# Sample cross-attention on four 32-column quarters of TensorE, two heads at a time

## The reference, cut to what matters

```python
D_MODEL, SEQ, DEPTH, DEC_BATCH, DEC_SEQ = 1024, 256, 2, 8, 8
N_MEM, XA_HEADS, XA_HEAD_DIM = 256, 4, 256

def cross_attend(h, mem_k, mem_v, w_q, w_o):
    b, L, _ = h.shape
    q = (h @ w_q).reshape(b, L, XA_HEADS, XA_HEAD_DIM)
    s = jnp.einsum('blhd,bmhd->bhlm', q, mem_k).astype(jnp.float32) * (XA_HEAD_DIM ** -0.5)
    p = jax.nn.softmax(s, axis=-1).astype(mem_v.dtype)
    o = jnp.einsum('bhlm,bmhd->blhd', p, mem_v).reshape(b, L, D_MODEL)
    return o @ w_o
```

## Time and profile before

| | |
|---|---|
| median of 3 runs | 2010.04 us (2007.63 to 2014.47) |
| profiled execution | 2015.52 us, of which the span 2013.6 us |
| mean granted TensorE clock in it | 0.933 of 2.4 GHz |
| PE busy | 1895.2 us (94%) |
| DMA | 382.66 MB, mean 190 GB/s |

### The profile page before, as it was taken

How to read it: one execution, slowest core, us unless ns; L and a number is a source line. 1 busy time by engine, 2 the same in 40 slices (tenths; PEclk the granted TensorE clock), 3 DMA queues, 4 the chain that set the end, 5 groups by cost and what they waited for, 6 DMA issues and landing times.

```text
span 2013.6 us, 18677 instructions
## 1 busy us (share of the span) xinstructions
PE 1895.2 (94%) x7908; PEld 1165.9 (58%) x7908; DVE 504.6 (25%) x1062; ACT 301.0 (15%) x666; POOL 32.1 (2%) x34
## 2 busy tenths in 40 slices
PE   7999999999999989999899999999999989999996
PEld 5766676666666534444367666766766664444342
DVE  0028544421102111111201276345011030211112
ACT  2114210311111010000111132104012011000001
POOL 0000000001000000000000000000010000000000
PEclk9999999899998689998999999999999967999898
DMA  6332226532453377877822422265325425887683
GB/s 253 125 114 99 84 105 221 213 141 94 164 216 122 135 283 310 329 321 292 334 71 101 163 87 71 97 235 224 131 99 209 167 84 208 331 332 298 270 324 143
DMA packets 28680, 382.66 MB, mean 190 GB/s; under 512 B 3184, under 2 KB 3568, under 8 KB 3888
## 3 DMA queue, kind: packets, MB, share of 16 engines
q1 hardware_dynamic: 25040, 356.69, 45.9%
q0 software_dynamic: 3552, 24.71, 3.0%
HBM read 356.67 MB, written 24.71 MB: 189 GB/s over the span
## 4 chain that ended last, share of the span: by engine, by line
PE 87%; DVE 4%; ACT 4%; DVEq 2%; issue 1%; DMA 1%; ACTq 0%; POOL 0%; SPq 0%; POOLq 0%
PE psum L471 27%; PE psum L925 11%; PE psum L910 7%; PE psum L945 7%; PE psum L749 7%; PE psum L970 4%; PE psum L808 3%; PE psum L838 3%; PE psum L478 2%; PE psum L712 2%; PE psum L689 2%; PE psum L709 2%; DVE work L1452 2%; PE psum L699 2%; PE psum L876 1%
## 5 line engine op out<-in xcount | busy, mean ns | idle before, releaser
L471 PE MATMUL psum<-h,ring 128*128 128x320 f32 x1920 | 535.2, 439 | 7.7 <-DVE h L1377 6.3
L471 PEld LDWEIGHTS psum<-h,ring 128*128 128x128 f32 x1920 | 367.9, 193 | 165.3 <-issue 18.0
L925 PE MATMUL psum<-ring,work 128*64 128x512 f32 x1024 | 237.6, 609 | 1.5 <-ACT work L1325 1.4
L925 PEld LDWEIGHTS psum<-ring,work 128*64 128x64 f32 x1024 | 70.4, 139 | 142.3 <-issue 136.8
L910 PE MATMUL psum<-work 128*128 128x128 f32 (+1 forms) x768 | 150.4, 329 | 1.4 <-ACT work L1312 1.4
L910 PEld LDWEIGHTS psum<-work 128*128 128x128 f32 (+1 forms) x768 | 114.1, 204 | 55.4 <-issue 29.4
L945 PE MATMUL psum<-ring,work 128*64 128x512 f32 x512 | 142.2, 718 | 1.1 <-ACT work L1337 1.1
L749 PE MATMUL psum<-work,ring 128*128 128x320 f32 x512 | 138.3, 433 | 0.9 <-ACT work L1099 0.9
L471 PE MATMUL psum<-mem,ring 128*128 128x256 f32 x512 | 122.8, 394 | 4.0 <-ACT work L1099 4.0
L749 PEld LDWEIGHTS psum<-work,ring 128*128 128x128 f32 x512 | 97.1, 190 | 42.0 <-ACT work L1099 1.8
L471 PEld LDWEIGHTS psum<-mem,ring 128*128 128x128 f32 x512 | 98.4, 197 | 21.2 <-issue 7.1
(11 more groups left out here) (240 smaller groups left out, 1453.2 us busy)
## 6 DMA issues: line engine op xcount, KB each, us to landing
ring<-stream SPq DMA_DIRECT2D x168, 2048.0 KB, 9.0
st_out<-states_out POOLq DMA_DIRECT2D x18, 1024.0 KB, 9.4
mk_out<-k_mem POOLq DMA_DIRECT2D x2, 1024.0 KB, 6.1
mv_out<-work POOLq DMA_DIRECT2D x2, 1024.0 KB, 5.6
cst<-consts SPq DMA_DIRECT2D x1, 1456.0 KB, 22.0
x<-x_in SPq DMA_DIRECT2D x1, 1280.0 KB, 5.8
y_out<-h POOLq DMA_DIRECT2D x2, 640.0 KB, 3.2
mem<-mem_in SPq DMA_DIRECT2D x1, 1024.0 KB, 23.9
```

The costliest lines, as they stand in the source:

```text
L471: mm = pe.matmul(out, w[:, a:a + P], rhs[:, j, :], start=(j == 0), stop=(j == KD - 1))
L925: mm = pe.matmul(psum[ab * CAP:(ab + 1) * CAP, up, :], h_packed[:, p % 2, k, ab * CAP:(ab + 1) * CAP], w[:, a:a + BANK], start=(k == 0), s ...
```

## The change

The eight batches become two groups (`GB`) of four. Batch b of a group is multiplied by 8 stationary columns straight from the queries, and its result goes to PSUM rows 32b to 32b + 7, that is to the b-th quarter of 32 columns of the array; `q_own`, `prob_own` and POOL's two memsets go. Each group is treated as a tile of 128 tokens in softmax and in the transposes (`XT` = 4 tiles: two of the prompt, two of the sample). The stage is cut in two halves `hp` of two heads each, and the stream is ordered to match: `Q_MQ` = 24 and 27, `Q_KC` = 25, 26, 28, 29. Queries use PSUM banks 4 to 7, so the wait for the copied values (`s_vtout`) now stands ahead of them. DVE, not ACT, now copies transposed probabilities and the transposed output.

```diff
-Q_MQ = 24
-Q_KC, Q_VC = 26, 30
+Q_MQ = [24, 27]
+Q_KC, Q_VC = [25, 26, 28, 29], [30, 31, 32, 33]
...
@@ PE (removed: L766 to L852, but for this wait) @@
                 pe.wait_ge(s_vtout, (L + 1) * 4)
+                def queries(hp):
+                    for c in range(4 * hp, 4 * hp + 4):
+                        w = quad(pe, L, Q_MQ[hp])
+                        if c >= 4:
+                            pe.wait_ge(s_qout, L * KD + c - 3)
+                        products(psum[:, 4 + c % 4, 0:T], w, (c % 4) * SLAB, P, h,
+                                 L * NNORM + 1 if c == 0 else None).then_inc(s_q, 1)
+                    free(Q_MQ[hp])
+                def scores(hp):
+                    pe.wait_ge(s_qout, L * KD + 4 * hp + 4)
...
+                    for gb in range(GB):
+                        q = Q_KC[2 * hp + gb]
+                        w = quad(pe, L, q)
+                        if hp == 1:
+                            pe.wait_ge(s_xexp, L * 8 + 2 + gb + 1)
+                        for rr in range(2):
+                            for c in range(2):
+                                k = 2 * (2 * hp + rr) + c
+                                for b in range(4):
+                                    own = SEQ + (4 * gb + b) * DS
+                                    a = ((b * 2 + rr) * 2 + c) * M
+                                    mm = pe.matmul(psum[32 * b:32 * b + DS, 2 + gb, rr * M:(rr + 1) * M],
+                                                   q_all[:, k, own:own + DS], w[:, a:a + M],
+                                                   start=(c == 0), stop=(c == 1))
...
+                        free(q)
+                def turn_probs(hp):
+                    for i in range(XT):
+                        u = 4 * hp + i
+                        pe.wait_ge(s_prob, L * 8 + u + 1)
...
+                        for rc in range(4):
+                            mm = pe.transpose(psum[:, 4 + i, rc * P:(rc + 1) * P],
+                                              prob[:, i, 2 * hp + rc // 2, (rc % 2) * P:(rc % 2 + 1) * P], ident)
...
+                def prompt_out(hp):
+                    for j in range(4 * hp, 4 * hp + 4):
+                        pe.wait_ge(s_ptout, L * 8 + 4 * hp + max(2, j % 4 + 1))
...
+                def sample_out(hp):
+                    pe.wait_ge(s_ptout, L * 8 + 4 * hp + 4)
+                    for gb in range(GB):
+                        q = Q_VC[2 * hp + gb]
+                        w = quad(pe, L, q)
...
+                        for rr in range(2):
+                            for c in range(2):
+                                for b in range(4):
+                                    own = SEQ + gb * P + 32 * b
+                                    a = ((b * 2 + c) * 2 + rr) * DV
+                                    mm = pe.matmul(psum[32 * b:32 * b + DS, 2 * hp + gb, rr * DV:(rr + 1) * DV],
+                                                   prob_t[:, 2 * hp + rr, c, own:own + DS], w[:, a:a + DV],
+                                                   start=(c == 0), stop=(c == 1))
...
+                        free(q)
+                def turn_out(hp):
+                    for gb in range(GB):
+                        pe.wait_ge(s_otok, L * 4 + 2 * hp + gb + 1)
+                        transposes([(psum[:, 2 * hp + gb, i * P:(i + 1) * P],
+                                     o_tok[:, gb, (4 * hp + i) * P:(4 * hp + i + 1) * P])
+                                    for i in range(4)]).then_inc(s_ott, 1)
+                queries(0)
+                scores(0)
+                queries(1)
+                scores(1)
+                turn_probs(0)
+                prompt_out(0)
+                sample_out(0)
+                turn_probs(1)
+                sample_out(1)
+                prompt_out(1)
+                turn_out(0)
+                turn_out(1)
+                pe.wait_ge(s_xoout, (L + 1) * KD)
+                pe.wait_ge(s_ottout, (L + 1) * 4)
...
@@ ACT @@
+                        act.activation(q_all[:, c, :], psum[:, 4 + c % 4, 0:T], ACT.Copy).then_inc(s_qout, 1)
...
+                queries(0)
                 exps(0)
+                queries(1)
                 exps(1)
+                prompt_out(0)
+                sample_out(0)
+                sample_out(1)
+                prompt_out(1)
...
@@ DVE @@
+                maxima(0)
+                probabilities(0)
+                maxima(1)
+                turned_probs(0)
+                probabilities(1)
+                turned_probs(1)
+                turned_out(0)
+                turned_out(1)
...
@@ POOL @@
-                pool.memset(q_own[:], 0.0).then_inc(s_qzero, 1)
-                pool.memset(prob_own[:], 0.0).then_inc(s_pzero, 1)
```

More of the change, by code:

```diff
@@ L214, in build @@
         v_mem = view(work, 0, 2, D)
[L215 to L222, removed]
+        q_all = view(work, 2048, KD, T)
+        prob = view(work, 4608, XT, XH, M)
+        prob_t = view(work, 8704, XH, 2, XT * P)
+        o_tok = view(work, 12800, GB, D)
+        xmax = view(work, 14848, 2 * XT, 2)
+        xsum = view(work, 14864, 2 * XT, 2)
         chosen = view(work, 0, PAIRS, 3, 2 * CAP)
@@ L765, in attention @@
                     mm.then_inc(s_vt, 1)
[L766 to L774, removed]
@@ L784, in attention @@
                                 first(mm)
[L785 to L800, removed]
@@ L803, in attention @@
[L803 to L819, removed]
@@ L820, in attention @@
[L820 to L844, removed]
-                        mm.then_inc(s_xo, 1)
-                    if b % 2 == 1:
-                        free(Q_VC + b // 2)
@@ L848, in attention @@
[L848 to L852, removed]
+                        mm.then_inc(s_xo, 1)
+                def sample_out(hp):
[3 more added lines that the diff above has]
+                        w = quad(pe, L, q)
+                        pe.wait_ge(s_xexp, L * 8 + 4 + 2 * hp + gb + 1)
+                        for rr in range(2):
+                            for c in range(2):
+                                for b in range(4):
[3 more added lines that the diff above has]
+                                                   prob_t[:, 2 * hp + rr, c, own:own + DS], w[:, a:a + DV],
+                                                   start=(c == 0), stop=(c == 1))
+                                    if rr + c + b == 0:
+                                        first(mm)
+                        mm.then_inc(s_xos, 1)
+                        free(q)
@@ L1248, in attention @@
                                    ACT.Copy).then_inc(s_vtout, 1)
[L1249 to L1265, removed]
+                def queries(hp):
+                    for c in range(4 * hp, 4 * hp + 4):
+                        act.wait_ge(s_q, L * KD + c + 1)
+                        act.activation(q_all[:, c, :], psum[:, 4 + c % 4, 0:T], ACT.Copy).then_inc(s_qout, 1)
@@ new lines, in exps @@
+                def exps(hp):
+                    for i in range(XT):
+                        u = 4 * hp + i
+                        act.wait_ge(s_xmax, L * 8 + u + 1)
+                        for rr in range(2):
+                            act.activation(prob[:, i, 2 * hp + rr, :], psum[:, i, rr * M:(rr + 1) * M], ACT.Exp,
+                                           bias=xmax[:, u, rr:rr + 1], scale=1.0 / 16,
+                                           accum_out=xsum[:, u, rr:rr + 1])
+                        act.drain().then_inc(s_xexp, 1)
@@ new lines, in prompt_out, with sample_out @@
+                def prompt_out(hp):
+                    for j in range(4 * hp, 4 * hp + 4):
+                        act.wait_ge(s_xo, L * KD + j + 1)
+                        act.activation(h[:, j, 0:SEQ], psum[:, 4 + j % 4, 0:SEQ], ACT.Copy).then_inc(s_xoout, 1)
+                def sample_out(hp):
+                    for gb in range(GB):
+                        act.wait_ge(s_xos, L * 4 + 2 * hp + gb + 1)
+                        act.activation(o_tok[:, gb, hp * BANK:(hp + 1) * BANK], psum[:, 2 * hp + gb, :], ACT.Copy)\
+                            .then_inc(s_otok, 1)
@@ L1694, in probabilities @@
-                def probabilities(t):
-                    n = TOKN[t]
-                    dve.wait_ge(s_xexp, L * 3 + t + 1)
-                    dve.reciprocal(xsum[0:n, t, :], xsum[0:n, t, :])
-                    dve.drain()
-                    dve.tensor_tensor(prob[0:n, t], prob[0:n, t],
-                                      xsum[0:n, t, :].unsqueeze(2).broadcast_to([n, XH, M]), ALU.mult)\
-                        .then_inc(s_prob, 1)
-                for t in range(2):
-                    maxima(t)
@@ L1705, in attention, with maxima @@
-                for t in range(2):
-                    probabilities(t)
-                maxima(2)
-                probabilities(2)
+                def maxima(hp):
+                    for i in range(XT):
+                        u = 4 * hp + i
+                        dve.wait_ge(s_xs, L * 8 + u + 1)
```

(25 more changed lines are left out.)

70 lines of the change are left out of this document (31 added, 39 removed).

## The result

The changed kernel takes 1952.74 us (median of 4 runs, 1950.53 to 1957.21) against 2012.26 us (4 runs, 2007.63 to 2016.66): ratio 0.9707, 95% interval 0.9677 to 0.9737. Forecast were 1945 us, minus 65; measured is minus 59.5.

What follows compares the result with a forecast made beforehand. PE's program order was taken to bound the kernel. Minus 33.5 us for the stage plus 1.0 for the value wait is minus 32.5 a layer, minus 65 in all: 1945 us, likeliest range 1934 to 1957.

Steps and rivals of the forecast that it cites:

- A: Rival for the sample matmuls: quarters overlap only in pairs, 3.5 us a quad, 1969 us in all; chance 0.13.
- C: Rival for the sample matmuls: quarters do not overlap at all, 7.0 us a quad, 2024 us; chance 0.05.
- The 1.55 us: Threshold for four matmuls on the four quarters that decides for no overlap; 0.43 expected, 1.74 with none.
- The 33.5 us: Forecast saving per layer from the end of query chunk 4 to the output projection: 61.2 instead of 94.7 us.
- right for layer 1 too: Claim that the one-layer timeline from query chunk 4 to the output projection, 94.7 us before, also holds for layer 1.
- At 0.109 us a pass ... this is 10.5 us: Transposes of probabilities and output on PE: 10.5 us a layer against 3.5 before, plus 7.
- 33 ... lands at 50.5 to 50.8. PE waits 0.8: Sample output of heads 2 and 3: quad 33, issued at 42.7, lands at 50.5 to 50.8; PE waits 0.8 us.
- D: Rival: DMA becomes the bound where a slot comes free late (27, 33); plus 10, 1955 us; within the forecast's 0.66.
- Wait for the copied values: Wait now ahead of the queries: costs 1.0 us a layer, bounds 0.5 and 2.2, including possible low clock.
- rival B: Clock falls: five times a layer 1962 us, transposes only 1955 (chance 0.10 together); lasting low 2007 (chance 0.02).
- It costs nothing; without the queries above it, it would cost some 8 us: First softmax on DVE and ACT, under the queries of heads 2 and 3: costs nothing there, some 8 us uncovered.
- 2.38 times for three column tiles: Skill's overlap figure for sample matmuls; the same share for four tiles would give 17.6 us a layer, about 1950 us.

Runs made afterwards that it cites:

- doubled transposes: Changed kernel with the 16 transposes of the probabilities of heads 2 and 3 made twice in each layer; 1947.3 us, ratio 0.9692.
- further execution: The changed kernel run and profiled once more, with no edit; 1954.4 us, ratio 0.9719.
- half transfers: Changed kernel with the eight key and value quads of a layer bringing only half their bytes; 1937.1 us, ratio 0.962.
- both repaired kernels: Changed kernel with values through banks 0 and 1 and heads 2 and 3's prompt output before sample output: 1943.9 us; also with turn_out(0) before sample_out(1): 1939.8 us.

## Why the prediction was right, point by point

The mechanism and the size of the gain were right: PE's program order sets the time, four quarters run at once, and this alone is worth it (one, two, four quarters). Rivals A and C are out: a quad takes 1.8 us, with a mean of 379 ns for a pass as before. (The 1.55 us at which C was to decide come to 1.52 by the prediction's own terms; nothing rests on it.) The 33.5 us forecast for the stage from chunk 4 were 33.2 in layer 0 and 30.0 in layer 1. But the terms of the sum were off, and in part cancelled: in layer 0 the 4.6 us too many for transposes stand against 2.5 too few for quad 33 and 1.6 for a low clock that was not in the sum. So the 33.2 of layer 0 is partly luck, and "right for layer 1 too" did not hold.

*"At 0.109 us a pass ... this is 10.5 us"* was mis-sized. I took two passes for every fp32 matmul. A transpose has one: 16 transposes stand as x16 in 1.97 us, and before, eight stood as x8 in 1.03, which I had to hand. The three blocks take 5.85 us, not 10.5.

*"33 ... lands at 50.5 to 50.8. PE waits 0.8"* was the second mis-sized term. The cheap transposes helped PE to come 1.5 us sooner in layer 0 and 0.6 in layer 1. The quad was issued at 42.0 and 42.9, near the 42.7 forecast, but took 9.60 and 10.85 us to land instead of about 8: at 51.6 and 53.8. So 3.28 and 4.53 us of wait. The ring's transfers in the chain that ended last, quads 27 and 33 of each layer, and PE behind quad 33 in layer 1:

```profile
503.67 7.64 DMA ring<-stream
544.92 9.60 DMA ring<-stream
1462.81 8.56 DMA ring<-stream
1504.99 10.85 DMA ring<-stream
```

```profile
1515.88 3.60 PE L850 MATMUL psum<-ring,work 128*8 128x256 f32 x32 [4.53 <-DMA ring<-stream]
1519.41 4.73 PE L832 MATMUL psum<-work 128*128 128x256 f32 x16
```

The doubled transposes show that the first error mostly flowed into this wait: what PE saves ahead of a transfer it must wait for is worth nothing. From quad 30 on the transfers queue; two windows of the kernel after, the first at 403 GB/s:

```profile
536.00:561.00 25.00, 20.10 (x206) 13.10 (x195) 8.80 (x18) 6.77 (x19) 0.00 (x0) 0.93 0.99 403
523.10:530.10 7.00, 6.47 (x25) 4.41 (x24) 0.00 (x0) 0.87 (x2) 0.00 (x0) 1.00 0.00 0
```

Ahead of that DMA idles for 7 us (the second row): all three slots hold quads 27, 28 and 29, and no slot comes free until the queries of heads 2 and 3 are done. So I take it that the ring's depth and its order bind, with the bandwidth behind them; this is read from the rows, as no run had a deeper ring. D of the rivals ("a slot comes free late") was the right mechanism with a part of its size.

*Wait for the copied values: "I take 1.0"* was mis-sized. It cost a later start (1.1 and 0.8 us) and 1.1 and 1.4 us of lower clock: 2.2 a layer, my upper bound. Moving the banks got it back.

*The clock* (rival B) fell once more in each layer: behind the wait for quad 33, for 3.4 us in layer 0 and 6.8 in layer 1. The waits were longer than the ones for which I had ruled it out. It cost 0.8 us on the prompt output of layer 0 (4.54 against 3.72) and 0.8 on the passes ahead of it (2.74 against 1.91); in layer 1 it cost 1.0 and 1.7. It did not fall in the blocks of transposes, neither in the 2.0 us ones here nor in the 3.7 us ones of the doubled transposes, in agreement with the row at 190 us. The Trainium skill (TensorE: Matmul & The Clock Gate, Part 4), which I had cited, says that a transpose does not count as busy PE in the same way; the measurements here do not bear this out.

*"It costs nothing; without the queries above it, it would cost some 8 us"*: nothing is right, the 8 us are wrong. Four tiles follow each other, so only the first tile's delay could be bare, and the second half of the scores covers it. Two of the four terms from which I worked it out, 0.2 and 0.9, stand in no row that I named.

The Trainium skill's 2.38 times for three column tiles (TensorE: Matmul & The Clock Gate, Part 3) is a smaller share of the ideal than the runs show in a steady stream. In this kernel it is 0.218/0.057 = 3.8 times for four.

Open stays why transfers take longer in layer 1. Not only quad 33, with the same transfers queued ahead of it, differs (9.6 and 10.9 us): quad 27, with none in flight ahead of it, took 7.64 and 8.56, and quad 30 took 7.59 and 9.20. The further execution has 7.75 and 8.54 for quad 27 and 7.61 and 8.55 for quad 30, but nearly the same for quad 33 (9.77 and 9.80). With the values' banks moved, quad 27 differs again (7.62 and 8.61), the other two do not (7.75 and 7.60; 9.71 and 9.72).

## What to carry to other kernels

When small matmuls share PE by column quarters, let the inner loop run over the quarters, and count what feeds them: the stage here went from 55% to 80% DMA with three slots, and of the 28 us of passes that the step from two quarters to four takes away in the two layers, 16 were lost: 11 in waits for quads 27 and 33 and 4 at the low clock behind quad 33. Count passes by the row of the same kind of instruction, not by the data type. Once a transfer is the last thing awaited, look for work that can be put into the wait, and keep copies out of banks that the next section writes, as a late start can bring a stretch of low clock with it.

## What the runs showed of the hardware

- Passes on one, two and four column quarters: 0.218, 0.111, 0.057 us each at 256 columns, fp32.
- PE looks ahead over a bounded number of matmuls: with four matmuls in a row on each quarter, 64 passes took 8.0 us, between 3.6 (quarters in turn) and 14.0 (one quarter). A pass on another quarter started while four passes of the quarter before were still to come.
- A transpose of 128x128 in fp32 is one pass, 16 of them in 1.97 us (0.12 each); an fp32 matmul is two.
- A transfer of 2 MB issued with none in flight landed 7.6 to 7.8 us later in layer 0 and 8.5 to 9.2 in layer 1 (quads 27 and 30 of the changed kernel, two executions); those issued into the queue (quads 28, 29 and 31 to 35) took 8.4 to 14.2. One of 1 MB with none in flight took 5.3 us (quad 30 of the half transfers, layer 0).
- The clock fell for 6.8 us at the start of the queries when they began 1 us later, and in one layer did not fall at all when they began 1.5 us earlier again. Both are tendencies over layers (17 of 18, 6 of 6 in chunks 1 to 4), not a rule for one run. In the profiled executions of both repaired kernels it also fell at the start of the projection of layer 1 (36.38 us instead of 34.69).
